# Attention output rows: four transposes at a time, twice a head, instead of one in every step

## The chip, the core and the metric

The kernel runs on one core of a Trainium2 chip. Its engines run beside each other, each through its own queue in order: TensorE (PE: matmuls and transposes), VectorE (DVE), ScalarE (ACT), GpSimd (POOL) and SyncE (SP, which issues transfers). They meet through semaphores. The metric is the device time of one execution in microseconds (us); less is better. PE writes only to PSUM, which has eight banks of 512 float32 columns on each of 128 partitions.

## What is computed

One decoder layer on a sequence of 1024 tokens with 1024 channels, in float32. The change lies in the attention, cut from the reference:

```python
sc = jnp.einsum('bhcqd,bhckd->bhcqk', q_blk, kt).astype(jnp.float32)
sc = jnp.where(causal, sc, -jnp.inf)
p = jax.nn.softmax(sc, axis=-1)
p_diff = p[:, :, 0] - lam * p[:, :, 1]
o = jnp.einsum('bhqk,bhkv->bhqv', p_diff.astype(vt.dtype), vt)
...
o = rms_norm(o, subln_g) * (1.0 - lambda_init)
```

There are 8 heads; each has two score maps over 64 channels, whose softmaxes are subtracted, and values of 128 channels. The normalised rows `o` are needed transposed (channels on the partitions) for the product with `w_attn_proj` that follows. Around it stand the input projections, a gated short convolution, a pooling mixer, the merge of the three and a SwiGLU layer.

## The kernel before

A float32 operand is kept as two parts, high and low, and a product is three matmuls (PASSES, high x high, high x low, low x high). The high part is made by ACT (a copy that rounds), the low part by DVE (the source minus the high part).

A head is eight steps, step i for query block i of 128 rows. `step_of` is written out once for each engine, with the same steps; the order of an engine's work is the order of the calls in it. Blocks pass through the steps as through a pipeline. In step i:

- PE: the scores of block i (`scores`, L1866), into banks 0 to 3; the transposes of the difference of block i-1 (`diff_transposed`, L1792, i blocks of 128 columns: the first four in bank 4, the rest in bank 5); a quarter of a projection for the next head (`proj_part`, L1850); the product of block i-2 with the values (`weighted_values`, L1888 and L1890) into bank 6; and the transpose of the normalised output row of block i-4 (`y_transposed`, L1792) into bank 5.
- DVE: the mask on the scores (L1287), two maxima (L1290), the normalised row of block i-3 (`y_row`, L1298), the low part of the transposed difference (`pt`, L1188), the difference itself (L1277, L1278, `diff` L1280), in some steps a low part of weights (`ring`), of values (`vh`, step 4) or of the projection (`kt`, `qt` L1261, odd steps), the sum of the output row of block i-2 (`u_row`, L1305), and the low part of the transposed row (`y_out`, L1188).
- ACT: the high part of the transposed difference (`pt`, L677), the exponentials (`e_t`, L795), the other high parts, half of the output row (`u_lo`), the high part of the transposed row (`y_out`), and the sum of squares of the row (`junk_o`, L813). POOL makes the scale from it (`o_scale`, L546 to L548).

Banks 4 and 5 are handed over with two pairs of semaphores: PE raises `tr_done` for a bank after the last transpose of a group, ACT copies, DVE copies and raises `tr_free`, and PE waits for `tr_free` before it writes the bank again. Bank 5 (index 1) carries in a head four groups of the difference (of blocks 4 to 7, thus in steps 5, 6, 7 and in step 0 of the next head) and eight of single output rows, 12 = TT + TT // 2 in all. The scores of step i wait for the exponentials of step i-1, since they use the same banks. POOL stores a head's `y_out` when its last row has been copied, in step 3 of the next head.

The first head, the loop over six heads (two to a turn), the last head and four further steps that drain the pipeline (with a projection of the gates on PE) stand behind each other. `y_row` has two slots of 128 columns.

Of the kernel before, what the change touches and what calls it, by code (L numbers as in the profile page):

```python
# [6 lines left out]
F32 = mybir.dt.float32  # L7
# [5 lines left out]
P = 128  # L13
HALF = 512
# [3 lines left out]
HH, LL = 0, 1  # L18
# [54 lines left out]
def build(nc, x, g_pre_mix, w_in, b_gate, lambda_q1, lambda_k1, lambda_q2, lambda_k2, subln_g,  # L73
# [4 lines left out]
    HV = 2 * HD  # L78
    HEADS = w_attn_proj.shape[1] // HV
# [3 lines left out]
    TT = S // P  # L83
# [14 lines left out]
    with ctx:  # L98
# [8 lines left out]
        RF = R2 + 65536  # L107
        RRAW = RF + 32768
        RRING = RRAW + 8192
        RT = RRING + 16384  # L110
# [4 lines left out]
        def at(name, shape, dt, offset):  # L115
            return nc.alloc_sbuf_tensor_at(name, shape, dt, offset=offset)
# [39 lines left out]
        v_raw = at("v_raw", [P, TT, HV], F32, RF + 24576)  # L156
        y_row = at("y_row", [P, 2, HV], F32, RF + 28672)
        junk_o = at("junk_o", [P, HV], F32, RF + 28672 + 1024)
# [62 lines left out]
        ps = ctx.enter_context(nc.psum_tensor("ps", [P, 8, 512], F32))  # L221
        TB = (4, 5)
        U_BANK, PROJ_BANK = 6, 7

# [235 lines left out]
        def _(pool):  # L460
# [91 lines left out]
            def store_y(par, h):  # L552

                pool.wait_ge(tr_free[1], heads_out.at(1) * (TT + TT // 2) + TT)
                pool.dma_start(y_dram[bass.ds(h, 1)].rearrange("a p c -> (a p) c"),
                               y_out[:, par].rearrange("p s t -> p (s t)").bitcast(F32)).then_inc(y_stored[par], 16)
                heads_out.next()
# [71 lines left out]
            pool.wait_ge(tr_free[0], TT + HEADS * TT + 4)  # L629
            pool.wait_ge(tr_free[1], TT + HEADS * (TT + TT // 2) + 4)  # L630

# [6 lines left out]
            whole(s_raw[4][:, HH], 1, 0)  # L638
            pool.wait_ge(tr_free[1], TT + HEADS * (TT + TT // 2) + TT)
            whole(s_raw[1][:, HH], 1, 1)  # L640
# [30 lines left out]
        def _(act):  # L671
# [25 lines left out]
            def transposed_hi(b, dst, blocks=4):  # L697
                wait_apart(act, act_passed, tr_done[b], tr[b].at(1))
                copy(dst, ps[:, TB[b], 0:P * blocks].rearrange("p (k t) -> p k t", t=P)).then_inc(tr_hi, 1)
                tr[b].next()  # L700
# [115 lines left out]

            def y_hi(par, i):

                if i == 0:

                    heads_out.next()
                    act.wait_ge(y_free, heads_out.at())
                transposed_hi(1, y_out[:, par, HH, P * i:P * (i + 1)].rearrange("p (k t) -> p k t", t=P), 1)

# [7 lines left out]
            def step_of(par, i, lag=0, first=False, last=False):  # L832
# [24 lines left out]
                if lag < 3 and not (first and i < 2):  # L857
                    take_u_lo((i - 2) % TT)
                if not (first and i < 4):
                    y_hi(par if i >= 4 else 1 - par, (i - 4) % TT)  # L860
                if lag < 3 and not (first and i < 2):
# [9 lines left out]
            for i in range(TT):  # L871
                step_of(0, i, first=True)
            with turns(act, (HEADS - 2) // 2, {n: 4, r: 4, p: 8, t: 16, tr[0]: 16, tr[1]: 24, heads_in: 2, heads_out: 2}):
                for par in (1, 0):
                    for i in range(TT):
                        step_of(par, i)
# [17 lines left out]
            gates_half(3, 1)  # L894
            act.wait_ge(tr_free[1], TT + HEADS * (TT + TT // 2))
            with turns(act, (KT - 4) // 2, {n: 2, r: 2, g: 4}) as it:
# [278 lines left out]
        def _(dve):  # L1175
# [118 lines left out]
            def y_of(i):  # L1294

                dve.wait_ge(o_scaled, t.at(-2))

                dve.scalar_tensor_tensor(y_row[:, i % 2, :], u_row[:, i % 2, :],  # L1298
                                         o_scale[:, i % 2:i % 2 + 1], g_sub[:, :], ALU.mult, ALU.mult)\
                    .then_inc(y_ready, 1)  # L1300
# [5 lines left out]

            def y_lo(par, i):
                transposed_lo(1, lambda s: y_out[:, par, s, P * i:P * (i + 1)].rearrange("p (k t) -> p k t", t=P), 1)

            def step_of(par, i, lag=0, first=False, last=False):  # L1310
# [22 lines left out]
                if lag < 3 and not (first and i < 2):  # L1333
                    sum_u((i - 2) % TT)
                if not (first and i < 4):
                    y_lo(par if i >= 4 else 1 - par, (i - 4) % TT)
                t.next()
# [8 lines left out]
            for i in range(TT):  # L1346
                step_of(0, i, first=True)
            with turns(dve, (HEADS - 2) // 2, {n: 4, r: 4, p: 8, t: 16, trs: 40, step: 48, heads_in: 2}):
                for par in (1, 0):
                    for i in range(TT):  # L1350
                        step_of(par, i)
# [186 lines left out]

            tr_first = TT + HEADS * (TT + TT // 2)
            dve.wait_ge(g2_landed, 32)  # L1540
# [222 lines left out]
        def _(pe):  # L1763
# [129 lines left out]

            def y_transposed(i):
                pe.wait_ge(y_ready, t.at(-3))
                transpose_rows(1, y_row[:, i % 2, :], 1)

            def step_of(par, i, lag=0, first=False, last=False):
# [18 lines left out]
                if lag < 3 and not (first and i < 2):  # L1917
                    weighted_values(par if i >= 2 else 1 - par, (i - 2) % TT, newer)
                if lag < 5 and not (first and i < 4):
                    y_transposed((i - 4) % TT)  # L1920
                t.next()
# [8 lines left out]
            for i in range(TT):  # L1930
                step_of(0, i, first=True)
            with turns(pe, (HEADS - 2) // 2, {n: 4, p: 8, t: 16, tr[0]: 16, tr[1]: 24, heads_v: 2}):
                for par in (1, 0):
                    for i in range(TT):
                        step_of(par, i)
# [228 lines left out]
```

## Time and profile before

| | us |
|---|---|
| median of 3 runs | 1899.48 (1896.77 to 1899.66) |
| profiled execution | 1897.34 |
| its span, first to last instruction | 1895.6 |
| PE busy | 1839.3 (97%) |
| DVE busy | 1019.1 (54%) |
| ACT busy | 637.2 (34%) |
| POOL busy | 195.1 (10%) |

The heads run from about 138 to 503 us, and the draining steps to 527 us. A row of the timeline is start, duration, engine, line, operation, output<-inputs, shape and count; in brackets at its end stands the time in which the engine was idle before it, and what released it. Matmuls are pipelined, so the rows of PE overlap by their modelled ends: the distance from start to start is what one costs in the queue. The same holds for the rows of DVE and ACT, where the end of one overlaps the next by some 0.07 us.

### The profile page before, as it was taken

What the parts mean: (1) busy time and instruction counts of PE and PEld (TensorE: products, weight loads), DVE (VectorE), ACT (ScalarE), POOL (GpSimd) and SP (SyncE); (2) the same over time, 40 slices, a digit from 0 to 9 for tenths busy, and PEclk for the clock granted to TensorE, in tenths of its full rate; (3) what the DMA queues carried; (4) which work ended last, traced back from release to release, by engine and by line L of the source; (5) the groups of instructions that cost most, each with busy time, mean ns of one, the idle gap of its engine ahead of it and who ended that gap; (6) DMA issues with size and microseconds to landing.
All of it is one profiled execution on the core that took longest, in us unless ns stands there. A gap on an engine that the chain in (4) does not pass through costs nothing. (4 is left out here: it accounts for less than half of the span.)

```text
span 1895.6 us, 25484 instructions
## 1 busy us (share of the span) xinstructions
PE 1839.3 (97%) x8808; PEld 1517.7 (80%) x8808; DVE 1019.1 (54%) x1594; ACT 637.2 (34%) x1243; POOL 195.1 (10%) x416
## 2 busy tenths in 40 slices
PE   6999999999999999999999999999999999999987
PEld 5877777777788888888888878788888888788876
DVE  4218888888612254322321455765554555567766
ACT  4216666666621132112112223333333333221221
POOL 2211111211110000000000012410000000000002
PEclk9999999999999999999999999999999999999999
DMA  6221111111161111111111422222221222233332
GB/s 215 90 56 34 57 57 56 56 56 45 56 244 56 39 56 45 46 56 45 55 45 45 133 89 89 78 72 96 74 92 67 97 74 94 100 126 124 115 122 89
DMA packets 129109, 153.41 MB, mean 81 GB/s; under 512 B 4800, under 2 KB 107712, under 8 KB 128016
## 3 DMA queue, kind: packets, MB, share of 16 engines
q1 hardware_dynamic: 114400, 97.27, 16.3%
q0 software_dynamic: 14352, 54.23, 7.9%
q10 hardware_dynamic: 288, 1.05, 0.2%
q8 instruction: 37, 0.61, 0.1%
q14 instruction: 32, 0.26, 0.0%
HBM read 120.02 MB, written 32.51 MB: 80 GB/s over the span
## 5 line engine op out<-in xcount | busy, mean ns | idle before, releaser
L1784 PE MATMUL ps<-xn,ring 128*128 128x512 f32 x1824 | 415.9, 389 | 0.0
L1784 PEld LDWEIGHTS ps<-xn,ring 128*128 128x128 f32 x1824 | 342.1, 188 | 71.3
L1784 PE MATMUL ps<-w_d,hn 128*128 128x512 f32 x1008 | 228.8, 389 | 0.0
L1188 DVE TENSOR_TENSOR ring<-raw,ring 128x1024 fp32r<-128x1024 f32 x76 | 96.5, 1269 | 245.8 <-ACT ring L677 245.5
L1784 PEld LDWEIGHTS ps<-w_d,hn 128*128 128x128 f32 x1008 | 189.2, 188 | 39.3
L1850 PE MATMUL ps<-xn,ring 128*128 128x512 f32 x864 | 214.2, 398 | 1.4 <-DVE qt L1261 1.0
L1850 PEld LDWEIGHTS ps<-xn,ring 128*128 128x128 f32 x864 | 158.3, 189 | 33.1 <-issue 1.1
L2051 PE MATMUL ps<-s_op,t_op_T 128*128 128x512 f32 x720 | 169.9, 389 | 0.0
L2051 PEld LDWEIGHTS ps<-s_op,t_op_T 128*128 128x128 f32 x720 | 135.1, 188 | 28.1
L677 ACT ACTIVATE ring<-raw 128x1024 fp32r<-128x1024 f32 x76 | 80.0, 1053 | 142.1 <-PE ps L1784 132.8
L1725 DVE TENSOR_TENSOR ff_sum<-ff_sum,ps 128x512 f32<-128x512 f32 x128 | 87.8, 686 | 52.6 <-PE ps L1784 52.6
L2051 PE MATMUL ps<-hn,t_op_B 128*128 128x512 f32 x480 | 115.1, 389 | 0.0
L2051 PEld LDWEIGHTS ps<-hn,t_op_B 128*128 128x128 f32 x480 | 90.1, 188 | 18.7
L795 ACT ACTIVATE e_t<-ps,neg_max 128x256 f32<-128x256 f32 (+7 forms) x128 | 94.1, 740 | 21.6 <-DVE neg_max L1290 20.9
L1784 PE MATMUL ps<-w_v,xn 128*128 128x512 f32 x384 | 91.5, 398 | 4.6 <-DVE xn L1188 4.6
L1188 DVE TENSOR_TENSOR t_op_B<-pair,t_op_B 128x512 fp32r<-128x512 f32 x60 | 41.4, 690 | 96.9 <-ACT t_op_B L677 96.9
L1290 DVE TENSOR_REDUCE neg_max<-ps 128x1 f32<-128x256 f32 (+7 forms) x128 | 90.9, 752 | 2.2
L1784 PE MATMUL ps<-w_o,ring 128*128 128x512 f32 x384 | 89.0, 391 | 1.6 <-issue 1.6
L1784 PEld LDWEIGHTS ps<-w_v,xn 128*128 128x128 f32 x384 | 73.2, 192 | 20.1 <-DVE xn L1188 5.0
L1784 PE MATMUL ps<-ya,ring 128*128 128x512 f32 x384 | 87.2, 389 | 0.0
L1188 DVE TENSOR_TENSOR t_op_T<-t_raw_T,t_op_T 128x512 fp32r<-128x512 f32 x80 | 54.9, 687 | 58.2 <-ACT t_op_T L677 58.2
L1784 PEld LDWEIGHTS ps<-w_o,ring 128*128 128x128 f32 x384 | 71.6, 188 | 16.7 <-issue 2.0
(189 smaller groups left out, 2489.2 us busy)
## 6 DMA issues: line engine op xcount, KB each, us to landing
raw<-in_w_in_dram SPq DMA_DIRECT2D x58, 512.0 KB, 4.0
pair<-in_w_gate_up_dram SPq DMA_DIRECT2D x20, 1024.0 KB, 5.3
raw_down<-in_w_down_dram SPq DMA_DIRECT2D x22, 512.0 KB, 3.2
raw_down<-hf_scratch SPq DMA_DIRECT2D x22, 512.0 KB, 3.2
hf_scratch<-hf_out POOLq DMA_DIRECT2D x40, 256.0 KB, 2.3
y_scratch<-y_out POOLq DMA_DIRECT2D x8, 1024.0 KB, 4.2
ya<-y_scratch POOLq DMA_DIRECT2D x8, 1024.0 KB, 13.6
v_scratch<-v_out POOLq DMA_DIRECT2D x16, 256.0 KB, 2.3
```

Of the source, the lines that this page charges most:

```text
L677: return act.activation(dst, src, ACT.Copy, **kw)
L795: act.activation(e_t[:, i % 2, c, 0:w], ps[:, 2 * c:2 * c + 2, :].rearrange("p a b -> p (a b)")[:, 0:w], ACT.Exp, bias=neg_max[:, i % 2, c ...
L1188: return dve.tensor_tensor(dst, src, hi.bitcast(F32), ALU.subtract)
L1290: dve.tensor_reduce(neg_max[:, i % 2, c:c + 1], ps[:, 2 * c:2 * c + 2, :].rearrange("p a b -> p (a b)")[:, 0:P * (i + 1)], AX_X, ALU.max, ...
L1725: done = dve.tensor_tensor(f, f, ps[:, g.slot(4), :], ALU.add)
L1784: last = pe.matmul(ps[:, bank, :], lhs, rhs, start=i == 0, stop=i == len(pairs) - 1)
L1850: last = pe.matmul(ps[:, proj_bank(first, half), :], ring[:, which, a, P * k:P * (k + 1)], xn[:, b, k, HALF * half:HALF * (half + 1)], sta ...
L2051: last = pe.matmul(ps[:, bank, :], t_op[name][:, a, k, :], block(b, k), start=opens and (k, a, b) == (0, HH, HH), stop=(k, a, b) == (3, LL ...
```

## The change

The output rows are no longer transposed one in every step. Rows 0 to 3 of a head are transposed together in step 1 of the next head, rows 4 to 7 in step 3, each as four transposes into the whole of bank 5, with one copy of 512 columns on ACT and one on DVE. In steps 1 and 3 the difference has at most four blocks and uses bank 4 only. Bank 5 now carries YT = TT // 2 + 2 = 6 groups a head, and the counts that engines wait for follow. `y_row` holds all eight rows and lies at another place. The diff, without the lines that only replace the counts:

```diff
-        y_row = at("y_row", [P, 2, HV], F32, RF + 28672)
+        y_row = at("y_row", [P, TT, HV], F32, RT)
...
+        YT = TT // 2 + 2
...
-            def y_hi(par, i):
-
-                if i == 0:
+            def y_hi(par, quarter):
+
+                if quarter == 0:
...
-                transposed_hi(1, y_out[:, par, HH, P * i:P * (i + 1)].rearrange("p (k t) -> p k t", t=P), 1)
+                transposed_hi(1, y_out[:, par, HH, HALF * quarter:HALF * (quarter + 1)]
+                              .rearrange("p (k t) -> p k t", t=P))
...
-                if not (first and i < 4):
-                    y_hi(par if i >= 4 else 1 - par, (i - 4) % TT)
+                if i in (1, 3) and not first:
+                    y_hi(1 - par, i // 2)
...
-                dve.scalar_tensor_tensor(y_row[:, i % 2, :], u_row[:, i % 2, :],
+                dve.scalar_tensor_tensor(y_row[:, i, :], u_row[:, i % 2, :],
...
-                if not (first and i < 4):
-                    y_lo(par if i >= 4 else 1 - par, (i - 4) % TT)
+                if i in (1, 3) and not first:
+                    y_lo(1 - par, i // 2)
...
-            def y_transposed(i):
-                pe.wait_ge(y_ready, t.at(-3))
-                transpose_rows(1, y_row[:, i % 2, :], 1)
+            def y_transposed(quarter):
+                pe.wait_ge(y_ready, t.at(-3 if quarter else -5))
+                transpose_rows(1, y_row[:, 4 * quarter:4 * quarter + 4, :].rearrange("p k t -> p (k t)"))
...
-                if lag < 5 and not (first and i < 4):
-                    y_transposed((i - 4) % TT)
+                if i in (1, 3) and not first:
+                    y_transposed(i // 2)
```

In the orders below `vh,pt` are the products with the values, `kt,qt` the scores, `diff` the transposes of the difference, and `tr_free1` is the semaphore that says bank 5 is free. The changed file has two to three more lines ahead of these places, so its line numbers are higher. The rows ISA and REGISTER_ALU work out the values that are waited for. PE's order at the change from step 5 to step 6 of the first head, before:

```order
L1890 MATMUL ps<-vh,pt 128x128
L1888 MATMUL ps<-vh,pt 128x256
L1890 MATMUL ps<-vh,pt 128x128
L1792 MATMUL ps<-ident,y_row 128x128 [waits tr_free1,y_ready]
L1866 MATMUL ps<-kt,qt 128x512 [waits exp_done]
L1866 MATMUL ps<-kt,qt 128x512 x11
L1792 MATMUL ps<-ident,diff 128x128 [waits tr_free0,diff_ready]
```

and after:

```order
L1893 MATMUL ps<-vh,pt 128x128
L1891 MATMUL ps<-vh,pt 128x256
L1893 MATMUL ps<-vh,pt 128x128
L1869 MATMUL ps<-kt,qt 128x512 [waits exp_done]
L1869 MATMUL ps<-kt,qt 128x512 x11
L1795 MATMUL ps<-ident,diff 128x128 [waits tr_free0,diff_ready]
```

The transpose of the row (L1792 on y_row), with its waits for the row and for bank 5, is gone from between the products and the scores.

PE at the end of step 1 and the start of step 2, first turn of the loop, before:

```order
L1888 MATMUL ps<-vh,pt 128x256
L1890 MATMUL ps<-vh,pt 128x128
L1792 MATMUL ps<-ident,y_row 128x128 [waits tr_free1,y_ready]
L62 ISA
L1866 MATMUL ps<-kt,qt 128x384 [waits exp_done]
L1866 MATMUL ps<-kt,qt 128x384 x5
L62 REGISTER_ALU [waits diff_ready]
```

and after:

```order
L1891 MATMUL ps<-vh,pt 128x256
L1893 MATMUL ps<-vh,pt 128x128
L1898 REGISTER_ALU
L1795 MATMUL ps<-ident,y_row 128x128 [waits tr_free1,y_ready]
L1795 MATMUL ps<-ident,y_row 128x128 x3
L62 ISA
L1869 MATMUL ps<-kt,qt 128x384 [waits exp_done]
L1869 MATMUL ps<-kt,qt 128x384 x5
L62 REGISTER_ALU [waits diff_ready]
```

One transpose of a row has become four there, ahead of the scores of step 2 (L1866 before, L1869 after).

DVE at the same place, before:

```order
L1261 SCALAR_TENSOR_TENSOR kt<-ps,kt 128x512 [waits proj_hi]
L1304 REGISTER_ALU
L1305 TENSOR_TENSOR u_row<-ps,u_lo 128x128 [waits u_lo_ready]
L1204 REGISTER_ALU
L1188 TENSOR_TENSOR y_out<-ps,y_out 128x128 [waits tr_hi]
L1285 REGISTER_ALU
L1287 TENSOR_TENSOR ps<-ps,mask 128x2x128 [waits scores_done]
L1184 REGISTER_ALU
L1290 TENSOR_REDUCE neg_max<-ps 128x1 [waits dve_step]
```

and after:

```order
L1263 SCALAR_TENSOR_TENSOR kt<-ps,kt 128x512 [waits proj_hi]
L1306 REGISTER_ALU
L1307 TENSOR_TENSOR u_row<-ps,u_lo 128x128 [waits u_lo_ready]
L1206 REGISTER_ALU
L1190 TENSOR_TENSOR y_out<-ps,y_out 128x512 [waits tr_hi]
L1287 REGISTER_ALU
L1289 TENSOR_TENSOR ps<-ps,mask 128x2x128 [waits scores_done]
L1186 REGISTER_ALU
L1292 TENSOR_REDUCE neg_max<-ps 128x1 [waits dve_step]
```

The copy of the transposed row (y_out) stands where it stood, behind u_row and ahead of the mask, and is four times as wide. In steps 0, 2 and 4 to 7 it is gone from this place.

## Rows read from the trace of the kernel before

**Rows 1.** Busy time by engine in one head (from:to, length, busy, clock, DMA).
```profile
277.85:324.62 46.77, 45.10 (x287) 36.90 (x286) 41.26 (x92) 29.74 (x83) 9.09 (x26) 1.00 0.17 57
```

**Rows 2.** Waits of PE: waiting line, releaser, us in total, times, longest.
```profile
PE ps L1792 <- DVE y_out L1188: 6.0, 15, 0.6
PE ps L1792 <- DVE diff L1280: 5.3, 8, 1.0
```

**Rows 3.** Timeline of PE, step 5 to step 0 of the next head.
```profile
299.12 0.66 PE L1792 MATMUL ps<-ident,diff 128*128 128x128 f32 x4
300.41 0.33 PE L1792 MATMUL ps<-ident,diff 128*128 128x128 f32 x1 [0.63 <-DVE y_out L1188]
...
304.43 1.49 PE L1866 MATMUL ps<-kt,qt 64*128 64x512 f32 x12
...
312.24 1.33 PE L1792 MATMUL ps<-ident,diff 128*128 128x128 f32 x7
313.32 3.02 PE L1850 MATMUL ps<-xn,ring 128*128 128x512 f32 x12
...
318.89 0.66 PE L1792 MATMUL ps<-ident,diff 128*128 128x128 f32 x4 [0.61 <-DVE diff L1280]
...
320.22 2.99 PE L1850 MATMUL ps<-xn,ring 128*128 128x512 f32 x12
```

**Rows 4.** Timeline of DVE in the same head, step 1 to step 7.
```profile
282.36 0.69 DVE L1261 SCALAR_TENSOR_TENSOR kt<-ps,kt 128x512 fp32r<-128x512 f32 x1 [0.18 <-ACT kt L677]
283.83 0.29 DVE L1305 TENSOR_TENSOR u_row<-ps,u_lo 128x128 f32<-128x128 f32 x1 [0.79 <-ACT u_lo L677]
...
284.37 0.43 DVE L1287 TENSOR_TENSOR ps<-ps,mask 128x256 f32<-128x256 f32 x1
...
293.42 0.68 DVE L1261 SCALAR_TENSOR_TENSOR kt<-ps,kt 128x512 fp32r<-128x512 f32 x1
294.02 0.28 DVE L1305 TENSOR_TENSOR u_row<-ps,u_lo 128x128 f32<-128x128 f32 x1
...
300.07 0.28 DVE L1188 TENSOR_TENSOR y_out<-ps,y_out 128x128 fp32r<-128x128 f32 x1
300.27 0.42 DVE L1287 TENSOR_TENSOR ps<-ps,mask 128x256 f32<-128x256 f32 x1
...
306.06 0.42 DVE L1287 TENSOR_TENSOR ps<-ps,mask 128x256 f32<-128x256 f32 x1
...
317.48 1.28 DVE L1280 SCALAR_TENSOR_TENSOR diff<-e_t,d_scale 128x1024 f32<-128x1024 f32 x1
```

**Rows 5.** Timelines of PE in the first head, of PE and of ACT at steps 1 and 2.
```profile
152.71 0.22 PE L1890 MATMUL ps<-vh,pt 128*128 128x128 f32 x1
152.86 1.25 PE L1866 MATMUL ps<-kt,qt 64*128 64x512 f32 x12
...
283.26 0.22 PE L1890 MATMUL ps<-vh,pt 128*128 128x128 f32 x1
283.32 0.29 PE L1792 MATMUL ps<-ident,y_row 128*128 128x128 f32 x1
283.54 0.79 PE L1866 MATMUL ps<-kt,qt 64*128 64x384 f32 x6
284.26 0.44 PE L1792 MATMUL ps<-ident,diff 128*128 128x128 f32 x2
...
281.73 0.60 ACT L677 ACTIVATE kt<-ps 128x512 fp32r<-128x512 f32 x1 [1.02 <-PE ps L1850]
...
284.82 0.38 ACT L677 ACTIVATE pt<-ps 128x256 fp32r<-128x256 f32 x1 [0.17 <-PE ps L1792]
```

**Rows 6.** Timeline of DVE in the last head, step 5.
```profile
485.54 0.43 DVE L1287 TENSOR_TENSOR ps<-ps,mask 128x256 f32<-128x256 f32 x1 [0.54 <-PE ps L1866]
```

**Rows 7.** Timeline of all engines in the draining steps 0 and 1.
```profile
512.65 0.29 DVE L1305 TENSOR_TENSOR u_row<-ps,u_lo 128x128 f32<-128x128 f32 x1 [3.92 <-ACT u_lo L677]
...
513.24 0.36 PE L1888 MATMUL ps<-vh,pt 128*128 128x256 f32 x1 [0.81 <-DVE y_out L1188]
```

More of the change, by code:

```diff
@@ L552, in store_y @@
             def store_y(par, h):
-                pool.wait_ge(tr_free[1], heads_out.at(1) * (TT + TT // 2) + TT)
+                pool.wait_ge(tr_free[1], heads_out.at(1) * YT + TT)
                 pool.dma_start(y_dram[bass.ds(h, 1)].rearrange("a p c -> (a p) c"),
@@ L629, in _ @@
             pool.wait_ge(tr_free[0], TT + HEADS * TT + 4)
-            pool.wait_ge(tr_free[1], TT + HEADS * (TT + TT // 2) + 4)
+            pool.wait_ge(tr_free[1], TT + HEADS * YT + 4)
             def whole(dst, kh, half):
@@ L638, in _ @@
             whole(s_raw[4][:, HH], 1, 0)
-            pool.wait_ge(tr_free[1], TT + HEADS * (TT + TT // 2) + TT)
+            pool.wait_ge(tr_free[1], TT + HEADS * YT + TT)
             whole(s_raw[1][:, HH], 1, 1)
@@ L872, in _ @@
                 step_of(0, i, first=True)
-            with turns(act, (HEADS - 2) // 2, {n: 4, r: 4, p: 8, t: 16, tr[0]: 16, tr[1]: 24, heads_in: 2, heads_out: 2}):
+            with turns(act, (HEADS - 2) // 2, {n: 4, r: 4, p: 8, t: 16, tr[0]: 16, tr[1]: 2 * YT, heads_in: 2, heads_out: 2}):
                 for par in (1, 0):
@@ L894, in _ @@
             gates_half(3, 1)
-            act.wait_ge(tr_free[1], TT + HEADS * (TT + TT // 2))
+            act.wait_ge(tr_free[1], TT + HEADS * YT)
             with turns(act, (KT - 4) // 2, {n: 2, r: 2, g: 4}) as it:
@@ L1305, in sum_u, with y_lo @@
                 dve.tensor_tensor(u_row[:, i % 2, :], ps[:, U_BANK, 0:HV], u_lo[:, :], ALU.add).then_inc(u_ready, 1)
-            def y_lo(par, i):
-                transposed_lo(1, lambda s: y_out[:, par, s, P * i:P * (i + 1)].rearrange("p (k t) -> p k t", t=P), 1)
+            def y_lo(par, quarter):
+                transposed_lo(1, lambda s: y_out[:, par, s, HALF * quarter:HALF * (quarter + 1)]
+                              .rearrange("p (k t) -> p k t", t=P))
             def step_of(par, i, lag=0, first=False, last=False):
@@ L1347, in _ @@
                 step_of(0, i, first=True)
-            with turns(dve, (HEADS - 2) // 2, {n: 4, r: 4, p: 8, t: 16, trs: 40, step: 48, heads_in: 2}):
+            with turns(dve, (HEADS - 2) // 2, {n: 4, r: 4, p: 8, t: 16, trs: 16 + 2 * YT, step: 48, heads_in: 2}):
                 for par in (1, 0):
@@ L1537, in residual @@
                 tile.next()
-            tr_first = TT + HEADS * (TT + TT // 2)
+            tr_first = TT + HEADS * YT
             dve.wait_ge(g2_landed, 32)
@@ L1931, in _ @@
                 step_of(0, i, first=True)
-            with turns(pe, (HEADS - 2) // 2, {n: 4, p: 8, t: 16, tr[0]: 16, tr[1]: 24, heads_v: 2}):
+            with turns(pe, (HEADS - 2) // 2, {n: 4, p: 8, t: 16, tr[0]: 16, tr[1]: 2 * YT, heads_v: 2}):
                 for par in (1, 0):
```

## The prediction

> **What bounds the kernel now.** Over the whole span TensorE (PE) is busy, so I read only the stretch that the change touches: the eight heads, about 138 to 527 us of the profiled execution. A steady head takes 46.77 us, of which PE is busy 45.10 and VectorE (DVE) 41.26 [rows 1]: by the busy share PE looks like the bound and DVE seems to have slack. The view of PE's waits says where PE stood: 6.0 us in 15 waits for the copy of the normalised rows (y_out L1188) and 5.3 us in 8 waits for the difference (diff L1280) [rows 2]. Matmuls are drawn with modelled ends that overlap, so an idle time can hide between them; I therefore read issue times in one steady head [rows 3]. Transposes in a run start 0.11 us apart ((0.66 - 0.33) / 3). In step 5 the bank-5 transpose could start at 299.12 + 4 x 0.11 = 299.56 and starts at 300.41: 0.85 lost. In step 7 seven transposes take 313.32 - 312.24 = 1.08 instead of 0.77: 0.31 lost. In step 0 of the next head eight take 320.22 - 318.89 = 1.33 instead of 0.88: 0.45 lost. That is 1.61 us a head, in eight heads some 12.5 us with the last steps' wait, and all of it is bank 5 that a single output row still occupies. It is the gain that the change looks to have.
>
> But who is late there? The timeline of DVE answers [rows 4]. From step 3 to step 0 of the next head DVE runs without a gap: y_out at 300.07, the next mask at 300.27, 0.20 us apart, although PE had gone on from the scores for that mask to the transposes at 299.12. In step 6 the scores end at 304.43 + 1.49 = 305.92 and the mask starts at 306.06. So in steps 3 to 7 PE waits because DVE is behind, and bank 5 is only the place where PE shows it. The next such place is the difference: at 318.89 PE waited 0.61 us for it, by itself [rows 3]. The head is thus a PE stretch (from the end of the difference of step 7 to the mask of step 2) and a DVE stretch (from that mask at 284.37 to the end of the difference at 317.48 + 1.28 = 318.76, 34.4 us).
>
> The trace also bears on a rule of the Trainium skill. Rows: four single copies cost DVE 4 x 0.20 us of queue, one of 512 columns 0.60 [rows 4], a gain only while DVE is what is late. The Trainium skill, page Perfetto Trace Analysis, section Optimizing Scalar/DVE Operations, says that grouping helps if the engine is saturated, and that where it is not but makes others wait, smaller instructions let work finish sooner. In steps 3 to 7 the first half speaks for the change; in step 1, where DVE idles, the second speaks against it, and the price worked out for part B below is what that half would cost here.
>
> **Part A, step 7's difference to the row transposes of step 1 (PE's stretch).** Removed: the 0.45 us for bank 5 in step 0, since no row transpose of step 7 holds it, and the single row transpose of step 0. With it the last product to the scores took 283.54 - 283.26 = 0.28 us, without it 152.86 - 152.71 = 0.15 [rows 5]: 0.13 saved. Nothing else is late there: DVE waits there for PE's products by way of ACT (0.79 us ahead of u_row at 283.83 [rows 4]). A = -0.58 us. There are 7 such crossings between heads: -4.1 us.
>
> **Part B, from those transposes to the mask of step 2.** Before: transpose at 283.32, scores at 283.54, ended at about 284.33, mask at 284.37: 1.05 us [rows 4, 5]. The copy of one row by ScalarE (ACT) and DVE ran under the scores. Now four rows go as one chain, and DVE takes the wide copy ahead of the mask, in its own order: transposes 0.66; to ACT 0.12 (284.26 + 0.44 = 284.70, copy at 284.82); ACT's copy of 512 columns 0.60; to DVE 0.03 (281.73 + 0.60, DVE at 282.36); DVE's 512 columns 0.60 until the next starts [rows 3, 4, 5]. Sum 2.01 us. PE's own way (0.32 more, so 1.37) is shorter. B = +0.95 us. No row shows this chain whole. Its ends are +0.32 (the chain hidden, PE alone) and +1.4 (each of the four hand-overs 0.1 longer); I take 0.95, as every link has a row. The cover it loses is the 0.79 us of scores. Queued behind the waiting copy on DVE are the mask, both maxima and so the exponentials of step 2; PE does not wait for these at once, but the DVE stretch starts later by all of it.
>
> **Part C, mask of step 2 to the end of step 7's difference (DVE's stretch).** Removed are the single copies of steps 2, 4, 5 and 6, at 0.20 each: -0.80. The copy of step 3 becomes the wide one: 294.02 - 293.42 = 0.60 against 0.20 [rows 4], +0.40. C = -0.40 us. PE's 1.16 us of waits in steps 5 and 7 lie inside this stretch and give nothing: PE reaches the scores 0.8 us sooner and finds the exponentials not done, or reaches the transposes and waits for the difference. The wait moves, it does not go. ACT loses six small copies and gains two wide ones; in this stretch it waits for DVE's maxima, so nothing comes of that.
>
> **The sum.** Head 1 has only the -0.60 of steps 4 to 6. Heads 2 to 7 have B + C = +0.55 each: +3.3. In the last head nothing is projected or split in steps 3 to 5, and PE is the bound again there (the mask at 485.54 waited 0.54 for PE [rows 6]); B is absorbed, I take -0.1. After the last head the projections of the gates run on PE: the wait of 0.81 us for y_out at 513.24 [rows 7] shrinks, but the products also need the row before it summed (u_row), which ended at 512.65 + 0.29 = 512.94, so PE gains 0.3 at most; and it issues three more transposes in each of two places, less the single ones: about as much. I take 0. Altogether -4.1 - 0.6 + 3.3 - 0.1 = **-1.5 us**. The profiled execution took 1897.34 us (its span is 1895.6), so it would take 1895.8; the median of the runs, 1899.48, lies 2.1 above it, and with the same difference gives 1898.0 us, 0.08% less. All that the change adds outside these parts is nothing: y_row lies elsewhere and eight rows deep, no transfer moves (the store of a head still follows step 3), and the granted clock is 1.00 through the heads [rows 1].
>
> **Rivals.** (1) PE's waits come back in full: -12.5 us, 1887 us. For it: PE is busy 96% of a head. Against it: DVE has no gap where PE waits. It holds only if DVE's work in steps 3 to 7 could start earlier, and DVE is released by itself there. (2) The chain of B is hidden, so B is +0.32: 6 x 0.63 = 3.8 less, 1894.2 us. For it: DVE waits 0.79 us in step 1 ahead of u_row [rows 4], so it is there in time. Against it: DVE takes its queue in order, with the wide copy ahead of the mask. (3) Slower: in steps 2 to 6 the removed small copies give nothing back, because the mask is then released by PE's scores (or the maxima by ACT) and not by DVE. The place is the mask of step 6, where the scores are only 306.06 - 305.92 = 0.14 us ahead [rows 3, 4]; it decides from the point at which PE does not gain the 0.2 us that DVE gains. Then C is +0.40 and head 1 gives nothing: 6 x 0.80 + 0.6 = 5.4 more, so +3.9 us, 1903.4. Against it: PE stands 0.85 us before that, in step 5, and loses that wait, so the scores should come earlier too.
>
> **How the numbers follow.** Forecast 69%: 1898.0, with the bounds of B and some 0.1 us a head on C from 1895 to 1901. Rival 1, 5%; rival 2, 12%; rival 3, 12%; something not in this list 2%. About 0.2%, 3.8 us, is what a measurement of this kernel can tell from no change. Rival 2 lies 5.3 below, so it counts as faster, with rival 1: 17%. Rival 3 lies on the edge, so half of it counts as slower, and with 3% for the forecast's own upper tail slower has 9%; the rest, 74%, is within. The range, 1894.0 to 1902.5, takes in rival 2 and the near side of rival 3 and leaves out rival 1 and the rest of rival 3; three runs of the same kernel already differ by 2.9 us.
>
> **What would show it.** In the changed kernel's waits, PE has none for y_out in steps 5, 7 and 0, and the sum of PE's waits for diff and the exponentials grows from 5 to 10 us or more. DVE still runs without a gap from step 3 to step 0. In step 1 the wide copy on DVE is idle before it for ACT, and the mask of step 2 starts 1.9 to 2.1 us after the first row transpose (before 1.05). A steady head takes 46.6 to 46.8 us as before (46.77). A steady head of 45.1 would mean rival 1, of 46.1 rival 2, of 47.4 rival 3. I am wrong if the mask of step 2 is not late, or if DVE shows gaps in steps 4 to 6.

## The result, and the profile after

The changed kernel took 1906.77 us (median of 7 runs, 1899.04 to 1908.52), the kernel before 1899.66 us on the same chip (7 runs, 1896.77 to 1901.92). The ratio is 1.0032, with a 95% interval of 1.0016 to 1.0048: slower by 0.3%, and above the forecast range of 1894.0 to 1902.5. (The ratios here and below are worked out over all runs, so they are not the quotients of the medians.) Below, this same kernel once more gave 1.0028. Three executions far outside all others, of 2822, 3081 and 6517 us, are left out of the figures of the experiments. The profiled execution is the shortest of the seven, 1899.04 us (the others took 1904.20 to 1908.52), so it shows only a part of the loss: from the difference of the first head to that of the last it takes 504.29 - 175.47 = 328.82 us, 3.5 more than before (502.82 - 177.47 = 325.35).

The page of the changed kernel, its span and its busy times: there is less work on DVE and ACT than before, and yet the span is longer.

```profile
span 1897.3 us, 25235 instructions
PE 1838.5 (97%) x8808; PEld 1521.8 (80%) x8808; DVE 1015.1 (54%) x1546; ACT 626.9 (33%) x1195; POOL 195.0 (10%) x416
```

Four heads from difference to difference, as in [rows 1] (stretch, us, busy time of PE, PEld, DVE, ACT and POOL with instructions, granted clock, DMA share, GB/s):

```profile
221.94:268.38 46.44, 44.61 (x286) 37.09 (x284) 40.76 (x86) 28.39 (x78) 9.05 (x26) 1.00 0.18 58
268.38:317.27 48.89, 46.34 (x286) 38.41 (x284) 40.71 (x85) 28.39 (x78) 9.05 (x26) 0.97 0.17 54
317.27:363.70 46.43, 44.61 (x286) 37.05 (x284) 40.76 (x85) 28.38 (x78) 9.05 (x26) 1.00 0.17 57
363.70:412.82 49.12, 46.31 (x286) 38.35 (x284) 40.71 (x85) 28.39 (x78) 9.05 (x26) 0.97 0.17 54
```

Most heads are a little shorter than before (46.44; the whole of before has 46.77 and 46.49 in turn, mean 46.6), where the sum had 0.03 less for each. Two of them, with the same work, take 2.5 and 2.7 us more, and their granted clock is 0.97. Nothing in the prediction has such heads.

What the prediction did speak of is there. DVE in one of the undisturbed heads, as in [rows 4]:

```profile
329.80 0.29 DVE L1307 TENSOR_TENSOR u_row<-ps,u_lo 128x128 f32<-128x128 f32 x1 [0.79 <-ACT u_lo L678]
330.66 0.69 DVE L1190 TENSOR_TENSOR y_out<-ps,y_out 128x512 fp32r<-128x512 f32 x1 [0.57 <-ACT y_out L678]
331.27 0.42 DVE L1289 TENSOR_TENSOR ps<-ps,mask 128x256 f32<-128x256 f32 x1
...
363.70 1.28 DVE L1282 SCALAR_TENSOR_TENSOR diff<-e_t,d_scale 128x1024 f32<-128x1024 f32 x1
```

and PE there, with its wait for the difference in the view of waits (us in total, times, longest), as in [rows 2, 3]:

```profile
329.29 0.62 PE L1795 MATMUL ps<-ident,y_row 128*128 128x128 f32 x4
```

```profile
PE ps L1795 <- DVE diff L1282: 12.8, 18, 1.4
```

The wide copy waits 0.57 us for ACT, and the mask of step 2 starts at 331.27, 1.98 us after the first row transpose. PE has no wait for y_out in the heads any more, and waits 12.8 us for the difference instead of 5.3.

The long heads differ from the others at their start. ACT of after, and behind it ACT of before, from the sum of squares of the row to the first copy of the transposed difference (`pt`), which is the first work of a turn of ACT's loop (one turn is two heads):

```profile
270.49 0.40 ACT L814 ACTIVATE junk_o<-u_row,rsums 128x128 f32<-128x128 f32 x1 [2.00 <-DVE u_row L1307]
270.80 0.18 ACT L814 ACTIVATION_READ_ACCUMULATOR junk_o<-u_row,rsums 128x1 f32 x1
275.30 1.09 ACT L678 ACTIVATE pt<-ps 128x512 fp32r<-128x512 f32 x2 [4.32 <-issue]
```

```profile
273.14 0.19 ACT L813 ACTIVATION_READ_ACCUMULATOR junk_o<-u_row,rsums 128x1 f32 x1
273.44 1.09 ACT L677 ACTIVATE pt<-ps 128x512 fp32r<-128x512 f32 x2
```

Before, ACT went over the jump without a pause. After, it stood 4.32 us, and the profile names no releaser ("issue"). In three other executions of kernels with the same pause it names the product of that step on PE (L1893, or L1897 where lines were added); ACT did not wait for that one, since here the copy starts at 275.30 and the last matmul of the product at 276.59. PE had started the transposes that it copies at 269.79, as its own row shows, with the wait for the difference ahead of them:

```profile
269.79 1.75 PE L1795 MATMUL ps<-ident,diff 128*128 128x128 f32 x8 [1.35 <-DVE diff L1282]
```

The copy comes 6.92 us after the start of the difference instead of 2.73. It is so at both inner jumps (7.18 us at the other) and at no crossing between two heads of one turn.

PE's granted clock in that stretch, three windows of after:

```profile
270.00:272.00 2.00, 2.00 (x10) 1.90 (x9) 1.28 (x5) 0.49 (x2) 0.71 (x2) 0.52 0.01 4
272.00:274.00 2.00, 2.00 (x7) 1.53 (x7) 0.35 (x1) 0.00 (x0) 0.95 (x3) 0.63 0.02 4
...
366.00:368.00 2.00, 2.00 (x7) 1.71 (x7) 0.95 (x4) 0.32 (x2) 0.93 (x3) 0.50 0.02 4
```

A granted clock of 0.5 is 1.2 GHz, one of 1.0 is 2.4; PE is busy in these windows all the time. Ahead of the first it stood 1.35 us in one piece for the difference; before, it stood 0.61 us for the difference and 0.45 for the bank, some transposes apart [rows 3], and every head had 1.00. So there are two suspects, and in this execution they lie on top of each other: **ACT's standstill** at the jump, and **the fall of the clock** behind PE's longer wait.

### The profile page after: what moved, and what is told of

It is laid out like the page before. It is cut to its first block and busy times, and to the rows that moved or that the text cites. A ratio compares the mean times of both kernels' runs of the same rounds, so it can differ in the third digit from the quotient of the medians.

```text
span 1897.3 us, 25235 instructions
## 1 busy us (share of the span) xinstructions
PE 1838.5 (97%) x8808; PEld 1521.8 (80%) x8808; DVE 1015.1 (54%) x1546; ACT 626.9 (33%) x1195; POOL 195.0 (10%) x416
```

## The experiments

Times are medians; the ratio is to the kernel before measured beside it, with its 95% interval. "+n" is the start of the first `pt` copy after the start of the difference. From the last difference of the heads to the end of the span the profiled executions take 1392.8 to 1397.7 us, in no order that follows the kernels (before 1392.8, and 1393.2 with ACT written out; the changed kernel 1393.0 and 1395.2). The time of one execution therefore does not tell such kernels apart; their heads do.

**The changed kernel again.**

> The changed kernel once more, as the measure for the runs beside it. Clock theory: its extra time over the kernel before comes in portions of about 2.5 us, one for each head crossing at which the granted clock falls after PE's wait of 1.36 us for the difference; so time and mean granted clock of a run go together: some 1894 to 1895 us with no fall (clock 0.994), 1904 to 1908 with four to six (0.990). Chain theory (the wide copies of step 1 cost the time): 1904 to 1908 in every run, whatever the clock.

Measured: 1903.83 us (7 runs) against 1898.21, ratio 1.0028 [1.0017, 1.0040]. The profiled execution has the two suspects apart:

```profile
222.60:270.60 48.00, 46.11 (x286) 38.45 (x284) 40.67 (x85) 28.57 (x78) 9.07 (x26) 0.96 0.17 56
270.60:319.80 49.20, 44.73 (x286) 37.06 (x284) 40.70 (x86) 28.45 (x78) 9.07 (x26) 1.00 0.17 54
```

The first is no start of a turn, has a clock of 0.96 and costs 1.6 us; the second starts a turn, has a clock of 1.00 and costs 2.8. They are two things. The other head that starts a turn takes 48.99 us here, also with a clock of 1.00; in the first execution the two took 48.89 and 49.12 with 0.97. So a fall of the clock behind the difference costs nothing where ACT stands still anyway.

**Useless matmuls ahead of the wait for the difference.** In `diff_transposed`, on the changed kernel; four in the first kernel, two in the second:

```diff
+                if i == TT - 1:
+                    wait_for(pe, tr_free[1], tr[1].at())
+                    for _ in range(4):
+                        pe.matmul(ps[:, TB[1], :], xn[:, HH, 0, 0:P], xn[:, HH, 0, 0:HALF], start=True, stop=True)
```

> The changed kernel with four matmuls of 512 columns without use, into bank 5, between the scores and the eight transposes of the difference in step 0 (0.94 us of PE work in the place where PE waits 1.36 us; bank 5 is overwritten by the transposes behind them). Clock theory: no fall of the clock in the heads, mean clock 0.994 as in the kernel before, 1893 to 1896 us, 10 us faster than the changed kernel beside it. Chain theory: as the changed kernel, 1905 to 1907, or slower by what the matmuls cost.

> As with four, but two matmuls (0.47 us), so that PE still waits some 0.9 us in one piece. Clock theory: fewer falls or none, 1893 to 1900 us, between the other two. Chain theory: as the changed kernel, 1905 to 1907.

Measured: 1903.86 us (ratio 1.0028 [1.0019, 1.0038]) with four and 1902.79 (1.0021 [1.0011, 1.0030]) with two, so the gain expected of the clock alone did not come. The heads of the kernel with four are 46.4 wherever no turn starts; the two others:

```profile
268.29:318.35 50.06, 47.21 (x291) 38.80 (x289) 40.77 (x85) 28.39 (x78) 9.04 (x26) 0.97 0.16 53
364.77:413.60 48.83, 45.85 (x291) 37.77 (x289) 40.68 (x86) 28.40 (x78) 9.05 (x26) 1.00 0.17 54
```

The standstill remains whole, and it can take the clock down by itself: in the first of these heads PE stood 2.13 us for the exponentials (until 277.26), and its clock is 0.50 from 278 to 280. Behind the wait for the difference the clock stays at 1.00 at every crossing.

**The kernel before, with the difference made late.** A DVE addition of 640 columns ahead of the last difference of a head:

```diff
+                if i == TT - 1:
+                    dve.tensor_tensor(late[:, :], e_t[:, b, 1, 0:5 * P], e_t[:, b, 0, 0:5 * P], ALU.add)
```

> The kernel before, rows transposed singly, with one more addition of 640 columns on DVE ahead of the difference of step 7 only (0.76 us until the next starts). PE's wait for the difference of 0.62 us then grows to about 1.38 us, as in the changed kernel, in a kernel that has none of the change. By itself that costs 8 x 0.76 = 6.1 us. Clock theory: the clock falls at head crossings, mean clock 0.992 or less, 6 us plus 2.5 us for each fall, 1908 to 1920. Chain theory: clock 0.994, 1905 to 1906.5.

Measured: 1909.24 us, ratio 1.0060 [1.0046, 1.0074], +11.0 us. Two heads, and PE at the start of the second:

```profile
223.51:270.75 47.24, 44.93 (x286) 36.87 (x284) 42.02 (x94) 29.87 (x83) 9.08 (x26) 1.00 0.18 57
270.75:319.30 48.55, 46.39 (x286) 38.00 (x284) 41.99 (x94) 29.98 (x83) 9.07 (x26) 0.96 0.17 55
```

```profile
272.16 2.03 PE L1795 MATMUL ps<-ident,diff 128*128 128x128 f32 x8 [1.37 <-DVE diff L1283]
```

An undisturbed head is 0.6 us longer than before (47.24 against the mean of 46.62), some 5 us in eight heads. Three of the seven heads have a clock of 0.96 and are 1.3 us longer again, which no head of the kernel before is: a one-piece wait of 1.37 us (1.29 at the last of the three) makes them here too, without anything of the change. The clock falls a fourth time behind the difference of the last head, after a wait of 1.75 us. The heads hold 8.0 us of the profiled execution's loss; the rest lies outside them.

**ACT's heads written out**, in the changed kernel and in the kernel before:

```diff
-            with turns(act, (HEADS - 2) // 2, {...}):
+            for _ in range((HEADS - 2) // 2):
```

> The changed kernel with ScalarE's work of the six middle heads written out instead of in a loop of three turns (the other engines keep their loops, and the work and its order are the same). In the profiled changed kernel ScalarE stood still for 4.4 us at the start of the second and of the third turn (its first copy came 6.9 and 7.2 us after the difference instead of 2.5), and those two heads took 2.5 us more. Turn theory: the standstill belongs to ScalarE's jump back, so it goes: all steady heads take 46.4 us, 4.9 us less in all, 1899 us at the median against 1904 of the changed kernel in the last comparison. Clock theory (falls of the clock at PE's wait of 1.36 us): unchanged, 1904 or more.

> The kernel before with ScalarE's heads written out in the same way. There ScalarE's first copy at the turns was late by 0.2 us only. Turn theory: nothing or up to 0.4 us less, 1898. If writing it out helped in general, for another reason, this one would gain 5 us too.

Measured: the changed kernel 1902.56 us, ratio 1.0012 [1.0002, 1.0021]; the kernel before 1899.14, ratio 1.0002 [0.9993, 1.0011]. The changed kernel lies between the two forecasts. Its copy now comes at +2.5 or +2.6 in each head, and what is left is the clock, at three of seven crossings:

```profile
222.84:270.87 48.03, 46.18 (x286) 38.45 (x284) 40.77 (x85) 28.61 (x78) 9.05 (x26) 0.96 0.17 56
270.87:317.29 46.42, 44.62 (x286) 37.03 (x284) 40.77 (x86) 28.40 (x78) 9.06 (x26) 1.00 0.17 57
```

A fall costs 48.03 - 46.42 = 1.6 us. For the kernel before, ACT's loop costs nothing.

**ACT's program padded with semaphore increments that nobody waits for**, so that its loop starts where it stood before and is as long. As the built programs count instructions, before has 278 ahead of the loop and 504 in it, the changed kernel 269 and 456.

```diff
+                elif not lag and not (first and i < 4):
+                    for _ in range(4 if not first and not last else 3 if first and i == 4 else 2):
+                        act.sem_inc(act_passed, 1)
```

> The changed kernel, with semaphore increments that nobody waits for put into ScalarE's heads where the small copies were, so that its first head has 278 instructions and its loop 504, as in the kernel before (269 and 456 in the changed kernel). If the standstill depends on the number of instructions in the loop or ahead of it, it is as in the kernel before: 46.4 us for every steady head, 1899 us. If it comes from something else that the change moved (when the engines arrive there), it stays: two heads of 48.9 us, 1904.

Measured: 1904.06 us, ratio 1.0021 [1.0011, 1.0031]. The time was missed, since three crossings had a fallen clock (48.1 us), but the mechanism was hit: no standstill, +2.5 to +2.7 in each head. With the 9 ahead alone, and with the 48 in the loop alone:

> The changed kernel with nine semaphore increments in ScalarE's first head and none in its loop: 278 instructions ahead of the loop as in the kernel before, 456 in it as in the changed one. If the place of the loop decides the standstill, it goes (steady heads of 46.4 us); if its length decides, it stays (48.9 us at the two turns).

> The changed kernel with 48 semaphore increments in ScalarE's loop and none ahead of it: 269 instructions ahead, 504 in the loop. If the length decides, the standstill goes; if the place decides, it stays.

Measured in one execution each, 1903.86 and 1907.97 us. ACT at the same jump, first of the kernel with 9 ahead, then of that with 48 in the loop:

```profile
273.54 1.08 ACT L678 ACTIVATE pt<-ps 128x512 fp32r<-128x512 f32 x2
```

```profile
276.75 1.08 ACT L678 ACTIVATE pt<-ps 128x512 fp32r<-128x512 f32 x2 [4.16 <-issue]
```

Where the loop starts decides, and not how long it is.

**Both causes taken away** (written out, two matmuls), and with that, or without the matmuls, **the first four rows transposed in step 2**, where their chain has other work beside it (PE's lines; the copies of ACT and DVE move in the same way):

```diff
-                if i in (1, 3) and not first:
-                    y_transposed(i // 2)
+                if i in ((1, 3) if lag else (2, 3)) and not first:
+                    y_transposed(i // 2 if lag else i - 2, -3 if i == 3 else -5 if lag else -6)
```

> ScalarE's heads written out, and two matmuls without use in PE's wait for the difference in step 0, which cuts it from 1.36 to 0.9 us in one piece. Both theories together: no standstill and fewer falls of the clock, mean clock 0.994 or more, 1895 to 1897 us. If the falls of the clock cost nothing by themselves, as the run with ScalarE written out alone.

> The changed kernel with ScalarE's heads written out, and the first four rows transposed in step 2 instead of step 1 (the others still in step 3). This tests part B: the chain of transposes and wide copies held the mask of step 2 for 1.98 us after the first row transpose. In step 2 DVE is busy when it comes, so the chain is hidden and only the wide copy itself (0.60 us) stands in DVE's queue. By the rows of the changed kernel the mask of step 2 comes 1.07 us earlier and DVE's stretch is 0.60 longer: 46.0 us for a steady head against 46.43, 6 x 0.45 = 2.7 us less than the run with ScalarE written out alone (1902.7), so 1900. If part B was mis-read, 46.4 and 1902.7.

> The same with the two matmuls without use in PE's wait of step 0: 46.0 us a steady head, hardly a fall of the clock at the crossings, 2.7 us less than 1898.3 of the run with steps 1 and 3: 1895.5 us, against 1899 of the kernel before.

Measured: 1898.26 us, ratio 0.9996 [0.9987, 1.0004]; 1896.1, ratio 0.9994 [0.9981, 1.0007]; 1893.6, ratio 0.9978 [0.9969, 0.9987]. The first is a little above its forecast of 1895 to 1897; the two others came out 4 and 2 us below theirs. The second kernel is uneven: three of its eleven runs took 1901.5 to 1904.8 us with a mean clock of 0.989 to 0.990, the others 1892.4 to 1896.8. A head of the first, then DVE and a head of the second, whose profiled execution has no fall of the clock in the heads although PE waits 1.36 us in one piece at six of the seven crossings:

```profile
267.46:313.90 46.44, 45.28 (x289) 37.36 (x287) 40.77 (x85) 28.42 (x78) 9.10 (x26) 1.00 0.17 57
```

```profile
331.20 0.68 DVE L1190 TENSOR_TENSOR y_out<-ps,y_out 128x512 fp32r<-128x512 f32 x1
331.80 0.42 DVE L1289 TENSOR_TENSOR ps<-ps,mask 128x256 f32<-128x256 f32 x1
```

```profile
267.49:313.53 46.04, 44.40 (x286) 37.01 (x284) 40.76 (x86) 28.79 (x78) 9.05 (x26) 1.00 0.17 57
```

In step 2 the wide copy has no idle time ahead of it, and the head loses 0.4 us. That much of part B was exposed and can be hidden by a step.

The four kernels of the changed order, by cause (ratios to before):

| | clock as it falls | two matmuls hold it |
|---|---|---|
| loop at 269 | 1903.83 (1.0028) | 1902.79 (1.0021) |
| written out | 1902.56 (1.0012) | 1898.26 (0.9996) |

The upper and the lower row were measured at different times, so only the ratios compare them. By the ratios the standstill taken away alone gives 0.16% (3.0 us) and the falls of the clock alone 0.07% (1.3 us, not clear of noise); as the second step they give 0.25% (4.7 us) and 0.16% (3.0 us; 4.3 by the medians of the lower row). Each ratio is known to 0.1%, so these totals do not show by themselves that the two overlap. The rows do: a head with the standstill takes 48.9 to 49.2 us at a clock of 1.00, and as much where the clock falls behind the difference. Only where it falls later, behind PE's wait for the exponentials, does the head take 50.1 us and more.

**What about the place of the loop?** The Trainium skill, page Runtime: NRT & Kernel Launch, section Instruction fetch mechanics, says that instructions are fetched in blocks of 256, and that a taken branch out of the blocks at hand has to wait for a fetch. Four further kernels put 256, 265, 4 and 244 increments ahead of the loop, in the first head (for 256, 32 in each of its eight steps):

```diff
+                elif first:
+                    for _ in range([32, 32, 32, 32, 32, 32, 32, 32][i]):
+                        act.sem_inc(act_passed, 1)
```

> The changed kernel with 256 semaphore increments more on ScalarE ahead of its loop over the six middle heads (32 in each step of the first head), so that 525 instructions stand ahead of the loop instead of 269; the loop itself is as in the changed kernel. Only the heads 2 to 7 are read (the first head may be longer, since ScalarE works through the increments there). The Trainium skill, page Runtime: NRT & Kernel Launch, section Instruction fetch mechanics, says that an engine's instructions are fetched in blocks of 256 and that a taken branch to a block that is no longer held must fetch it first. Theory P (the standstill depends on where the loop starts within such a block): 525 lies in its block where 269 lies, so the standstill is back as in the changed kernel, with the first pt copy about 6.9 to 7.2 us after the difference in the two heads that begin a turn (2 and 3), heads of 48.8 to 50.3 us, and 46.4 or 48.0 in the others. Theory T (any place from 278 on is free of it, as 278 was): pt copy at 2.7 us in every head, heads of 46.4, or 48.0 where the granted clock falls.

> The same with 265 increments, so that 534 instructions stand ahead of the loop, which is 278 plus 256. Theory P: no standstill, as with 278 ahead (pt copy at 2.7 us, heads 46.4, or 48.0 with a fall of the clock). Theory T: the same. If the standstill shows here too, the padding itself or the longer program makes it, and neither theory stands.

> The changed kernel with 4 increments ahead of the loop (273 instead of 269; 278 was free of the standstill). Only the edge is looked for. In the loop three instructions (register work and a wait) stand ahead of the first pt copy. If the end of a block lies within the loop's first few instructions and the standstill is the fetch of the block behind it (theory P), there is an edge between 269 and 278, and here the standstill is either whole (4.3 us) or gone, and nothing between. A theory by which the standstill grows slowly with the place (more instructions to fetch ahead of the copy) would give some 2 us of it here.

> The changed kernel with 244 increments ahead of the loop: 513 instructions ahead, which is 257 plus 256, 12 less within a block of 256 than the changed kernel. Theory P: the end of the block lies 12 instructions later in the loop, so the first pt copy is in time (2.7 us after the difference) and ScalarE stands still behind it instead, between the exponentials of step 0 and the first copies of step 1, until about 7 us after the difference; since the exponentials of step 0 or the copy behind them are late, the heads 2 and 3 that begin a turn are still longer than 46.4, by 1 to 3 us. Theory T: no standstill, heads 46.4 or 48.0. If there is a standstill ahead of the pt copy as in the changed kernel, the edge is a range of places, wider than the few first instructions.

Measured in one execution each, the same copy at the first jump of the kernels with 256, 265, 4 and 244 ahead, in that order:

```profile
277.56 1.08 ACT L678 ACTIVATE pt<-ps 128x512 fp32r<-128x512 f32 x2 [4.16 <-issue]
```

```profile
273.91 1.09 ACT L678 ACTIVATE pt<-ps 128x512 fp32r<-128x512 f32 x2
```

```profile
270.77 1.09 ACT L678 ACTIVATE pt<-ps 128x512 fp32r<-128x512 f32 x2
```

```profile
277.20 1.09 ACT L678 ACTIVATE pt<-ps 128x512 fp32r<-128x512 f32 x2 [2.32 <-issue]
```

| ahead of the loop | remainder by 256 | standstill at the first jump | us of the execution |
|---|---|---|---|
| 269 (after), 269 (48 more in the loop) | 13 | 4.3, 4.2 | 1899.04, 1907.97 |
| 525 | 13 | 4.2 | 1908.40 |
| 273 | 17 | none | 1898.59 |
| 278 (9 ahead) | 22 | none | 1903.86 |
| 534 | 22 | none | 1898.92 |
| 513 | 1 | 2.3 | 1905.27 |

The period of 256 holds at both places that it was tried: 256 instructions more bring the standstill back, 265 do not. Four instructions take all of it away, so the edge is sharp, between 13 and 17. The forecast for 513, no pause ahead of the copy but one behind it, failed: the pause is ahead of the copy, and half as long. So it is not shown that the end of a block must lie within the first few instructions of the loop.

The view of the transfers has queues for instructions. Their rows (packets, MB, share) from 262 to 450 us, a stretch with both inner jumps, first of the changed kernel and then of that with 4 ahead:

```profile
q14 instruction: 10, 0.08, 0.1%
q8 instruction: 1, 0.02, 0.0%
```

```profile
q8 instruction: 1, 0.02, 0.0%
```

Every kernel of the changed order in which ACT stands still has these ten packets of 8 KB on q14 (269, 513 and 525 ahead), and every one with the loop in which it does not (273, 278, 534) has none. The kernels with increments differ in nothing but these, on ACT, so the packets are ACT's. Three of them come at each jump. In the changed kernel they start at 271.5, 273.7 and 277.2 us, and the copy starts at 275.30, 1.6 us after the second; with 513 ahead they start at 275.4, 277.6 and 281.2, and the copy at 277.20, 1.8 us after the first. So ACT stands still while its instructions are fetched, for two packets with 269 ahead and for one with 513, which accounts for a pause half as long. This agrees with what that section of the Trainium skill says of a taken branch; why 269 needs the packets and 273 does not is not shown.

The kernel before has ten packets there as well, and they are not ACT's: with ACT written out there are 14, and the changed kernel written out has four. In the kernel before it is DVE that stands at its jump, at both inner jumps:

```profile
274.69 0.43 DVE L1287 TENSOR_TENSOR ps<-ps,mask 128x256 f32<-128x256 f32 x1 [1.69 <-issue]
```

It costs nothing: the head with this jump takes 46.77 us, the first head of the loop, with no jump, 46.75. In the changed kernel this pause of DVE is gone.

**Both causes away with the loop kept** (4 increments ahead, two matmuls), and with it the rows in step 2:

> The changed kernel with both suspected causes taken away without writing the loop out: 4 semaphore increments on ScalarE ahead of its loop over the heads (273 instructions ahead instead of 269) and two useless matmuls of 512 columns ahead of PE's wait for the difference at head crossings. If the place of the loop and the fall of the granted clock are the two causes and nothing else, the time is that of the kernel with ScalarE's heads written out and the same two matmuls, 1898.3 us, and every steady head takes 46.4 us; against the changed kernel with the two matmuls alone (1902.8) four instructions are then worth 4.5 us. If writing the heads out removed something else as well, it stays above 1900.

> The same with the first four rows transposed in step 2 instead of step 1, so that the chain of part B runs beside other work: what the grouping is worth when nothing disturbs it, still as a loop. Expected 1893.6 us as with ScalarE's heads written out, 0.2 to 0.3% under the kernel before, steady heads of 46.05 us. If the loop costs anything beyond its place, it lies above 1896.

Measured: 1897.64 us (11 runs), ratio 0.9993 [0.9984, 1.0002]; and 1893.0 us (6 runs), ratio 0.9972 [0.9960, 0.9984], against 1899.48. Both are as forecast. The first is not to be told from the kernel before by its time. A head of each:

```profile
268.36:314.80 46.44, 45.22 (x289) 37.34 (x287) 40.73 (x86) 28.50 (x78) 9.05 (x26) 1.00 0.17 56
```

```profile
268.16:314.21 46.05, 45.11 (x289) 37.37 (x287) 40.75 (x85) 28.98 (x78) 9.04 (x26) 1.00 0.18 57
```

Writing ACT's heads out did nothing that four instructions don't do. The last kernel, with the rows in step 2, is faster than the kernel before by 0.28%.

## Why the prediction was wrong

The sum over its own parts nearly held; what failed is the sentence behind it, "All that the change adds outside these parts is nothing", with "the granted clock is 1.00 through the heads".

- **Part A** (-0.58): from the end of the difference (317.27 + 1.28 = 318.55) to the first row transpose at 329.29 it is 10.74 us, before 11.34, so -0.60. Right.
- **Part B** (the mask 2.01 us after the first transpose): 1.98. Right, and it costs 0.93. Transposed one step later, the chain gives 0.4 us a head back, two thirds of the way to its bound of +0.32.
- **Part C** (-0.40): from the mask at 331.27 to the end of the difference at 363.70 + 1.28 it is 33.71 us, and so in every steady head. Before, it is 34.4 and 34.1 in turn (34.39 in the head that the prediction read), so -0.66 or -0.38, on average -0.52: the term was 0.12 too small. The steady head is 46.44, where 46.6 to 46.8 was forecast.
- **The sum** (-1.5 us): with both disturbances away and the loop kept, the stretch from the first head's difference to the last one's takes 323.64 us instead of 325.35, so -1.7. The terms of the sum for it give -4.1 + 3.3 - 0.1 = -0.9; C is most of the difference. The kernel takes 1897.64 us (1898.26 with ACT written out), close to the forecast of 1898.0, but its ratio of 0.9993 cannot be told from 1. The head shows the gain, the time of the kernel does not, and that it came so near is in part luck. This kernel is also not the one that was built.
- **The wait moves**: right, 12.8 us for the difference instead of 5.3. The failed step begins here. The prediction moved PE's waits together into one and gave that no price. Two short waits of 0.61 and 0.45 us became one of 1.35, and behind such a wait the clock fell at some crossings, 1.6 us each. That a wait of this size does so is shown by the kernel before with a late difference; that it is worth 3.0 us by the ratios (4.3 by the medians) in the absence of the standstill, by the table of four.
- **"Outside these parts is nothing"**: the four copies that ACT's first head lost moved the start of its loop from 278 to 269 instructions, and ACT stands 4.3 and 4.6 us at two jumps. With the clock held it is worth 0.25% (1.0021 against 0.9996) to 0.28% (against 0.9993 with four instructions ahead), some 5 us and more than all that the change gains. On ACT the trace of before shows nothing of it, since there its jump cost nothing; but DVE's 1.69 us of "issue" at its own jump was a sign that a jump can cost such a pause.
- **Rival 1** did not occur: PE's waits came back elsewhere, no steady head is 45.1. **Rival 2**, a head of 46.1, is what the kernel with the rows in step 2 shows (46.04, from a head that was shorter than forecast to begin with), not the change. **Rival 3** did not occur: C was larger than said, not smaller. The time of 1903 to 1907 us near its 1903.4 is a coincidence; DVE has no gaps in steps 4 to 6.
- **The chances**: slower had 9%, 6 of it from rival 3 and 3 from the forecast's own upper tail, and none from what happened. The 2% for "something not in this list" was far too little for a change that moves both a wait and the code of every engine.

What stays open: why the loop at 269 has its instructions fetched anew at each jump and the loop at 273 does not. Open too is why the clock falls at some crossings and at others with the same wait does not, and how the loss of an execution that was not profiled, 7 us at the median, divides among the causes: the two profiled executions of the changed kernel show 3.5 and 5.3 us of it in the heads.

## What to carry to other kernels

When waits on the engine that bounds a kernel are moved together, price the one longer wait as well, and look at the granted clock behind it: here it and the standstill turned a gain of 1.7 us in the heads into a loss. When an edit changes the number of instructions ahead of a long loop, compare the first instruction of its turns in both traces; if an engine stands there with no releaser, or with one that it does not wait for, look for packets on the instruction queue and try a few empty instructions ahead of the loop. Grouping copies helps on the saturated stretch and costs its chain elsewhere, so the group belongs in a step in which the copying engine has other work.

## What the hardware showed that was not expected

- A jump back in ACT's loop costs nothing or holds ACT up by several us, by the place of the loop's start: 4.2 to 4.6 us with 269 or 525 instructions ahead, 2.2 to 2.3 with 513, none with 273, 278 or 534. The pause goes with packets on the instruction queue, ten from 262 to 450 us against none.
- PE's granted clock fell to 1.2 GHz in a stretch in which PE is busy 96% of the time, at some crossings after a wait of 1.2 to 1.4 us, and at none after the 0.5 to 1.0 us of before and of the kernels with two matmuls. Each fall lengthens the head by 1.6 us (48.03 against 46.42), by 1.3 in the kernel before with a late difference. The Trainium skill, page TensorE: Matmul & The Clock Gate, section A second HAM failure mode: psum-queue depth-cycling, tells of short idle times between groups of matmuls that take the clock down again and again; the rows agree in kind.
- Two useless matmuls ahead of the wait are worth 3.0 us by the ratios (1.0012 against 0.9996 with ACT written out; the medians are 1902.56 and 1898.26): they shorten PE's wait for the difference from 1.36 to 0.70 us at a steady crossing.
